# A three-product float32 matmul: both parts of the operand in one product of 512 columns

## The reference

```python
proj = jnp.einsum('bsd,de->bse', h, w_in)                     # 2048 x 15424
q = jnp.einsum('bsr,re->bse', _rmsnorm(q_a, q_a_norm_g), w_q_b)
kv = jnp.einsum('bsr,re->bse', _rmsnorm(c_kv, kv_a_norm_g), w_kv_b)
y_mla = jnp.einsum('bse,ed->bsd', attn * jax.nn.silu(z_mla), w_o_mla)
y_conv = jnp.einsum('bse,ed->bsd', b_gate * conv * jax.nn.silu(z_conv), w_o_conv)
merged = jax.nn.sigmoid(g_mla) * y_mla + jax.nn.sigmoid(g_conv) * y_conv
out = jnp.einsum('bsd,de->bse', merged, w_out)
```

## Time and profile before

| | us |
|---|---|
| median of 3 runs | 2057.07 |
| the profiled execution | 2053.59 |
| its span | 2052.3 |
| TensorE busy in it | 1996.5 |
| TensorE's weight loads busy | 1935.6 |
| VectorE busy | 1167.2 |
| ScalarE busy | 876.5 |
| GpSimd busy | 298.5 |

### The profile page before, as it was taken

One profiled execution on the slowest core, in us unless ns is written; L12 is line 12 of the kernel. 1 busy time (PEld: TensorE's weight loads), 2 busy tenths in 40 slices (PEclk: granted clock), 3 DMA queues, 4 the chain that ended last, 5 costly groups with the idle time before them and its releaser, 6 DMA issues.

```text
span 2052.3 us, 37120 instructions
## 1 busy us (share of the span) xinstructions
PE 1996.5 (97%) x15778; PEld 1935.6 (94%) x15778; DVE 1167.2 (57%) x1727; ACT 876.5 (43%) x1264; POOL 298.5 (15%) x335
## 2 busy tenths in 40 slices
PE   7999999999999999999999699999999999999999
PEld 7999999999999999999999699898999988999987
DVE  5765555555554455644654655476456677564654
ACT  5444454444344334444444433345443333354443
POOL 2110010202010002300211521030011122030200
PEclk9999999999999999999999999999999999999999
DMA  7465454466666566565565364443464443556564
GB/s 238 142 189 174 139 149 144 135 185 184 185 178 185 185 184 180 179 188 184 185 223 183 118 203 134 132 136 113 145 185 134 124 124 115 175 183 190 184 227 159
DMA packets 177695, 343.79 MB, mean 168 GB/s; under 512 B 10478, under 2 KB 19050, under 8 KB 177002
## 3 DMA queue, kind: packets, MB, share of 16 engines
q1 hardware_dynamic: 176154, 337.16, 54.4%
q10 hardware_dynamic: 1376, 4.26, 0.6%
HBM read 335.09 MB, written 6.29 MB: 166 GB/s over the span
## 4 chain that ended last, share of the span: by engine, by line
PE 83%; issue 8%; DVE 2%; POOL 2%; ACT 1%; POOLq 0%; DVEq 0%; ACTq 0%
PE bank L1233 82%; DVE w_lo L1853 1%; POOL arena L2434 1%; ACT w_hi L1556 1%; POOL scratch L2431 1%; DVE arena L2120 0%; POOL arena L2478 0%; POOL stats L2385 0%; DVE head_factor L1890 0%; ACT scratch L1714 0%; DVE ob_lo L2125 0%; DVE arena L2222 0%; ACT ob_hi L1712 0%; POOL acc_a L2365 0%; DVE best L2220 0%
## 5 line engine op out<-in xcount | busy, mean ns | idle before, releaser
L1853 DVE TENSOR_TENSOR w_lo<-w_raw,w_hi 128x1024 fp32r<-128x1024 f32 (+2 forms) x644 | 784.5, 1222 | 800.8 <-ACT w_hi L1556 799.5
L1556 ACT ACTIVATE w_hi<-w_raw 128x1024 fp32r<-128x1024 f32 (+2 forms) x644 | 661.5, 1031 | 935.1 <-PE bank L1233 934.5
L1233 PE MATMUL bank<-hb_hi,w_hi 128*128 128x256 f32 x2448 | 700.1, 286 | 0.0
L1233 PE MATMUL bank<-hb_lo,w_hi 128*128 128x256 f32 x2448 | 694.9, 284 | 0.0
L1233 PE MATMUL bank<-hb_hi,w_lo 128*128 128x256 f32 x2448 | 694.7, 284 | 0.0
L1233 PE MATMUL bank<-ob_hi,w_hi 128*128 128x256 f32 (+1 forms) x2224 | 645.6, 290 | 11.3 <-DVE ob_lo L2125 7.1
L1233 PE MATMUL bank<-ob_hi,w_lo 128*128 128x256 f32 (+1 forms) x2224 | 628.0, 282 | 0.0
L1233 PE MATMUL bank<-ob_lo,w_hi 128*128 128x256 f32 (+1 forms) x2224 | 626.7, 282 | 0.0
L1233 PEld LDWEIGHTS bank<-hb_hi,w_hi 128*128 128x128 f32 x2448 | 471.5, 193 | 6.8 <-DVE w_lo L1853 5.4
L1233 PEld LDWEIGHTS bank<-hb_lo,w_hi 128*128 128x128 f32 x2448 | 471.6, 193 | 0.0
L1233 PEld LDWEIGHTS bank<-hb_hi,w_lo 128*128 128x128 f32 x2448 | 471.3, 193 | 0.0
(11 more groups left out here) (245 smaller groups left out, 1217.0 us busy)
## 6 DMA issues: line engine op xcount, KB each, us to landing
w_raw<-in_w_in SPq DMA_DIRECT2D x436, 512.0 KB, 3.7
w_raw<-in_w_out SPq DMA_DIRECT2D x64, 512.0 KB, 4.1
w_raw<-in_w_o_conv SPq DMA_DIRECT2D x32, 512.0 KB, 3.7
w_raw<-in_w_o_mla SPq DMA_DIRECT2D x32, 512.0 KB, 3.7
w_raw<-in_w_branch SPq DMA_DIRECT2D x32, 512.0 KB, 3.7
w_raw<-in_w_kv_b SPq DMA_DIRECT2D x16, 512.0 KB, 3.9
w_raw<-in_w_q_b SPq DMA_DIRECT2D x16, 384.0 KB, 3.3
arena<-x_kept SPq DMA_DIRECT2D x2, 2048.0 KB, 9.0
```

The lines of the kernel that those rows point to most:

```text
L1233: return nc.tensor.matmul(dst, lhsT, rhs, start=start, stop=stop, skip_group_check=True)
L1556: act(dst, src, ACT.Copy).then_inc(S_("w_hi"), 1)
L1853: tt(low, src, high.bitcast(F32), ALU.subtract).then_inc(S_("w_lo"), 1)
```

## The change

The two operand buffers `hb_hi`, `hb_lo` become halves of one buffer `hb`, likewise `ob`. In the phases marked `wide` (256 tokens and no `hold`) the products hi x hi and hi x lo of an f tile are one product of 512 columns: its moving side is 256 columns of the high part followed by the same 256 of the low part, and it fills a whole bank. The product lo x hi is added to the first half. Token-major tiles, the phases with 272 columns and wout stay. VectorE then adds the two halves of the bank (a TENSOR_REDUCE over pairs, which raises `sum`), waits for it, and multiplies in SBUF as before. `sum` frees the bank, `evac` starts what follows. Where the factor and the result are the same buffer (bgate, oconv, branch_a), the sum goes to a scratch buffer, taken from the ring of five.

```diff
+        self.wide = n == S and not hold
...
-        self.hb_hi, self.hb_lo = sb("hb_hi", [P, KT, S], F32R), sb("hb_lo", [P, KT, S], F32R)
-        self.ob_hi, self.ob_lo = sb("ob_hi", [P, KT, T], F32R), sb("ob_lo", [P, KT, T], F32R)
+        self.hb, self.ob = sb("hb", [P, 2, KT, S], F32R), sb("ob", [P, 2, KT, T], F32R)
+        self.hb_hi, self.hb_lo = self.hb[:, 0, :, :], self.hb[:, 1, :, :]
+        self.ob_hi, self.ob_lo = self.ob[:, 0, :, :], self.ob[:, 1, :, :]
...
+    def both(self, name, k):
+
+        if name in ("h", "mg", "ya", "yb"):
+            return self.hb[:, :, k + 8 * (name == "yb"), :]
+        if name == "h2":
+            return self.ob[:, :, k, NMETA:T]
+        return self.ob[:, :, k + 4 * (name == "lat_kv"), 0:S]
...
-            if kind == "f":
+            if kind == "f" and u.phase.wide:
+                mm(pair(dst), hi_w[:, k, COLS(j)], m.both(u.phase.operand, kt), first, last)
+                inst = mm(dst[:, 0:S], lo_w[:, k, COLS(j)], x_hi, False, last)
+            elif kind == "f":
...
+    def both_by(s, dst, factor, *marks, between=None):
+
+        b, at = m.proj[s.of["pb"]], dst if between is None else between
+        ve.wait_ge(*s.of["got"])
+        for mark in marks:
+            ve.wait_ge(*mark)
+        v.tensor_reduce(at, b.rearrange("p (h x) -> p x h", h=2), AX, ALU.add).then_inc(S_("sum"), 1)
+        ve.wait_ge(*s["sum"])
+        tt(dst, at, factor, ALU.mult).then_inc(S_("evac"), 1)
...
     def gate(s):
         name, k = s.args
         if name in ("gc", "gm"):
-            out_by(s, scratch_of(s), m.R, done["r1"])
+            both_by(s, scratch_of(s), m.R, done["r1"])
...
     def evac_oc(g, m, pb, got):
         k = 4 * g + m
-        done["yc", k] = add("oconv", k, marks="evac", pb=pb, got=got)["evac"]
-        return done["yc", k]
+        sc = scratch.take()
+        s = add("oconv", k, marks="sum evac", pb=pb, got=got, scratch=sc)
+        sc.ends(s["evac"])
+        done["yc", k] = s["evac"]
+        return s["sum"]
```

More of the change, by code:

```diff
@@ L468, in evac @@
             sc = scratch.take() if m else None
-            s = add("latent", which, m, marks="evac sq" + (" sq_acc" if m else ""), pb=pb, got=got, scratch=sc)
+            s = add("latent", which, m, marks="sum evac sq" + (" sq_acc" if m else ""), pb=pb, got=got, scratch=sc)
             if m:
@@ L526, in evac @@
         def evac(g, m, pb, got):
-            s = add("cin", j, m, marks="evac", pb=pb, got=got, free=list(conv_free[m]))
+            s = add("cin", j, m, marks="sum evac", pb=pb, got=got, free=list(conv_free[m]))
             done["cin", m] = s["evac"]
-            return s["evac"]
+            return s["sum"]
         return evac
@@ L534, in evac @@
             sc = scratch.take()
-            s = add("cgate", j, m, marks="evac tap0", pb=pb, got=got, scratch=sc, gate=done["cin", m],
+            s = add("cgate", j, m, marks="sum evac tap0", pb=pb, got=got, scratch=sc, gate=done["cin", m],
                     free=list(conv_free[m]))
@@ L547, in evac @@
         def evac(g, m, pb, got):
-            s = add("bgate", j, m, marks="evac conv_b", pb=pb, got=got, taps=done["taps", m])
+            sc = scratch.take()
+            s = add("bgate", j, m, marks="sum evac conv_b", pb=pb, got=got, taps=done["taps", m], scratch=sc)
+            sc.ends(s["evac"])
             done["conv_b", m] = s["conv_b"]
-            return s["evac"]
+            return s["sum"]
         return evac
@@ L556, in evac @@
             sc, hd = scratch.take(), heads.take()
-            s = add("zconv", j, m, marks="evac sig silu gated", pb=pb, got=got, scratch=sc, head=hd, y=done["conv_b", m])
+            s = add("zconv", j, m, marks="sum evac sig silu gated", pb=pb, got=got, scratch=sc, head=hd, y=done["conv_b", m])
             hd.ends(s["silu"])
@@ L587, in evac @@
             sc = scratch.take()
-            s = add("gate", name, k, marks="evac gate", pb=pb, got=got, scratch=sc, free=list(free))
+            s = add("gate", name, k, marks="sum evac gate", pb=pb, got=got, scratch=sc, free=list(free))
             sc.ends(s["gate"])
             done[name, k] = s["gate"]
-            return s["evac"]
+            return s["sum"]
         return evac
@@ L608, in evac @@
             sc, hd = scratch.take(), ring.take()
-            s = add("z_sig", name, k, marks="evac sig", pb=pb, got=got, scratch=sc, head=hd)
+            s = add("z_sig", name, k, marks="sum evac sig", pb=pb, got=got, scratch=sc, head=hd)
             def gate_y():
@@ L634, in evac @@
             sc = scratch.take()
-            s = add("merge", name, k, marks="evac merged", pb=pb, got=got, scratch=sc, gate=done[gate, k], other=done[other, k])
+            s = add("merge", name, k, marks="sum evac merged", pb=pb, got=got, scratch=sc, gate=done[gate, k], other=done[other, k])
             sc.ends(s["merged"])
@@ L790, in evac_qa2 @@
     def evac_qa2(g, m, pb, got):
-        s = add("qa2", 4 * g + m, marks="evac", pb=pb, got=got)
+        s = add("qa2", 4 * g + m, marks="sum evac", pb=pb, got=got)
         pending.append(qa_job(4 * g + m, s["evac"]))
-        return s["evac"]
+        return s["sum"]
     def token_major(name):
@@ L866, in evac_qb @@
         sc = scratch.take()
[L867 removed]
+        s = add("qb", k, marks="sum evac sig qb", pb=pb, got=got, scratch=sc)
         sc.ends(s["qb"])
         done["qb", k] = s["qb"]
[L870 removed]
+        return s["sum"]
     def recurrence(pr):
@@ L953, in evac_ba @@
         k = 4 * g + m
-        done["pa", k] = add("branch_a", k, marks="evac", pb=pb, got=got)["evac"]
-        return done["pa", k]
+        sc = scratch.take()
+        s = add("branch_a", k, marks="sum evac", pb=pb, got=got, scratch=sc)
+        sc.ends(s["evac"])
+        done["pa", k] = s["evac"]
+        return s["sum"]
     run(ph["ba"], evac_ba)
@@ L2029, in cin @@
         j, t = s.args
-        out_by(s, m.gate_t[:, t, :], m.RR, done["rr"], *[done[key] for key in s.of["free"]])
+        both_by(s, m.gate_t[:, t, :], m.RR, done["rr"], *[done[key] for key in s.of["free"]])
     def cgate(s):
         j, t = s.args
-        out_by(s, scratch_of(s), m.gate_t[:, t, :], s.of["gate"])
+        both_by(s, scratch_of(s), m.gate_t[:, t, :], s.of["gate"])
     def taps(s):
```

62 lines of the change are left out of this document (32 added, 30 removed).

## The result

The changed kernel takes 2164.3 us (median of 4 runs, 2163.5 to 2165.1) against 2056.3 before: 1.052 times, interval 1.051 to 1.054. The forecast was 2096. It has the sign right and the size wrong: 5.2% slower for 1.9%. The profiled span is 2163.6 us.

The account below looks back on a forecast made before the run. TensorE, busy 1996.5 of 2052.3 us, was taken to bound the kernel. Stalls of 74 us minus 33.3 saved gave +41, so 2094 from the profiled 2053.59 and, with the runs' median higher, 2096 us; range 2040 to 2165.

Parts of the forecast that it names:

- the gate group's 0.95 us of stall: At the ends of 12 gconv, gmla and gb groups TensorE stands 0.95 us for a late w_lo: 11.4 us.
- the wait for the third bank: In 24 groups without a sigmoid, the next group's fourth tile waits 0.4 us for the third tile's bank: 9.6 us.
- latents, qb: Four groups with ScalarE behind each evacuation: 4 us of stalls.
- saving of the products: On TensorE two products of 256 columns become one of 512; 4016 change, each saves 0.0083 us, together 33.3 us.
- the sum over the groups: Stalls from VectorE's longer evacuations, mostly at the ends of groups, added over all kinds of group: 74 us.
- z phases: zconv, zmla, zb, 10 groups: 0.95 us of stall plus 0.6 from a later w_lo beside GpSimd: 16 us.
- The recurrence: ga, za, ba, 10 groups mostly beside the recurrence: 1.7 us counted of a burst's 2.8 growth, 17 us.
- The clock: TensorE's granted clock was read as that of 2.4 GHz in all slices (digit 9).
- the third: Rival: VectorE's sum is dearer, 0.93 us, since it steps 256 elements; 66 us more, 2162; chance 0.20.
- The first: Rival: queues absorb the burst, as the sum costs no more than an evacuation now (0.41 us); 2036 us; chance 0.14.
- the second: Rival: gain and loss cancel; wide product at 0.2133 us, 74 us more, half given back; 2059; chance 0.05.
- the fourth: Rival: the wide product on TensorE brings nothing (0.240 us); 33 us more, 2128; chance 0.08.

Follow-up runs that it names:

- e1_products: Changed kernel's products, but the old one-operation evacuation, reading only the first half of the bank; 2034.4 us, 0.990 of the kernel before.
- e3_from_bank: As e4_bank_held, but the multiplication reads the bank's first half, so the sum is made but left out of the result; 2139.8 us, 1.041.
- e4_bank_held: As the changed kernel, but the bank is freed by the multiplication and not by the sum; 2171.0 us, 1.056 of the kernel before.
- e5_narrow_rec: As the changed kernel, but with the change taken back in ga, za and ba, the phases beside the recurrences; 2139.7 us, 1.041.

## Why the prediction was wrong

Right were: the pitch of the wide product in layer 1, the sum (0.68 us for 0.67), the evacuation's 1.06 us, the gate group's 0.95 us of stall, the wait for the third bank (0.57 for 0.4, oconv), VectorE's busy time, TensorE's waits for `w_lo` (53.8 us for some 50), and that a gain on TensorE is lost on VectorE at the ends of groups. Lateness against e1_products, by the kinds of the sum:

| kind | forecast | measured |
|---|---|---|
| gconv, gmla, gb | 11.4 | 17.0 |
| zconv, zmla, zb | 16 | 29.7 |
| cgate | 8 | 5.5 |
| latents, qb | 4 | 12.2 |
| cin, bgate, oconv, omla, bb, qi, qa2 | 9.6 | 20.0 |
| q | 8 | 12.4 |
| ga, za, ba | 17 | 29.8 |
| saving of the products | -33.3 | -21.6 |

The kinds of the table add up to 127 us; the other phases and the start bring it to 130.

The step that failed is the sum over the groups: 74 us of stalls, measured 130 in spans. The mechanism, a longer burst ahead of `w_lo` in strict queues, was right; four of its terms were too small, and the clock was put at nothing.

- **z phases, and what they hand on.** "Shifted, and with about 0.4 us because the multiplication now reads SBUF twice beside GpSimd": the mechanism was seen and counted once a group. It is paid at every meeting, three times 0.5 us in a zmla group. The second zmla group stood 4.3 us longer than with the products alone, for 1.6. The runs split this: 1.1 us are there without the slow multiplications (24.05 us in e3_from_bank against 22.98), 1.7 come with them (25.75 in e4_bank_held), and 1.6 with the lower clock, which e4_bank_held does not have there. The first gconv, gmla and gb groups carry some of the lateness: 23.72 us against 21.56 in gconv, while the inner groups stand 0.9 to 1.5 us for the forecast 0.95.
- **The recurrence.** "Of the 2.8 us that a burst grows I count 1.7: 17. Ends of this choice: 0 and 28." It was 29.8, just above my upper end; ga's groups stood 2.6 to 6.1 us each. I had bounded the term by the burst's growth. A step of the recurrence that starts late also leaves TensorE idle, and behind the idle the clock is lower. Here is the end of ga's last group, VectorE and then TensorE:

```profile
1735.65 0.42 DVE L1997 TENSOR_TENSOR scratch<-scratch,factor 128x256 f32<-128x256 f32 x1
1737.50 1.23 DVE L1877 TENSOR_TENSOR w_lo<-w_raw,w_hi 128x1024 fp32r<-128x1024 f32 x1 [1.43 <-ACT w_hi L1580]
1738.64 0.72 DVE L2339 COPY_PREDICATED arena<-small,bank 128x256 f32<-128x256 uint8 x1
```
```profile
1739.71 1.94 PE L1254 MATMUL bank<-arena 128*128 128x64 f32 x8 [4.12 <-issue]
1741.41 0.77 PE L1254 MATMUL bank<-ob,w_hi 128*128 128x512 f32 x1
1741.98 0.41 PE L1254 MATMUL bank<-ob,w_lo 128*128 128x256 f32 x1
1742.19 0.63 PE L1254 MATMUL bank<-ob,w_hi 128*128 128x512 f32 x1
1742.62 0.41 PE L1254 MATMUL bank<-ob,w_lo 128*128 128x256 f32 x1
```

  The burst, the sigmoids, `w_hi`, `w_lo` and only then the recurrence's own COPY_PREDICATED: TensorE's next product starts only behind that one and has stood 4.12 us.
- **Latents, qb, and the phases that wait for a bank.** 19 us more than forecast in the two kinds. The multiplications of the latents and of qb too meet GpSimd (6.5 us of e4_bank_held against e3_from_bank), and that was not costed. In oconv the wait for a bank came out near the forecast (0.57 us for 0.4); why cin, bgate and qa2 stand longer stays open, as do the 4 us by which q is over.
- **The products.** The saving was 0.0083 us each from one phase's pace, and 0.0054 in the mean: 12 us. Of the Trainium skill ("TensorE: Matmul & The Clock Gate", Back-to-back issue gap) the prediction gave the formula alone: the page calls it the gap of a product by itself and says that in a stream, where each product has its weight load, it is off in both directions. So it did not decide the matter; the measured mean lies between its 0.0025 us and my 0.0083.
- **The clock.** It was read as full from the digit 9 and put at nothing. The granted clock of the profiled execution is 0.979, and 0.991 in e1_products. I estimate what that costs from the products that start in the stretches at 1.2 GHz, at 0.417 us more for 1000 columns (the difference between the two levels): 31 us in the changed kernel, 13 in e1_products and 7 in the kernel before. So some 18 of the 130 us are the clock's; they lie inside the terms above and are not to be added to them.

56 us of stalls and 12 of saving make the 68 between 2096 and 2164. Of the rivals, the third gave 2162, near the measured time, for a reason that did not happen: its sum of 0.93 us was 0.68. It was luck, not a right rival. That the range reached just far enough (2165) is owed to that rival and supports no step. The first, queues that absorb the burst, was ruled out by the gate groups; the second (74 us saved) and the fourth (nothing saved) by the 21.6 us of e1_products.

## What to carry to other kernels

An operation added at an evacuation is paid where the queues are strict: ask what stands behind it on its engine, and if it is the feed of TensorE, issue only what frees the bank there and the rest behind the feed; the order alone gave back 87 of 108 us here. A cost met at every tile beside another engine is counted per meeting, not per group, and a pace taken from one phase is checked in each phase it is used for. Where a chain runs through several engines, a wait can cost more than its length: behind TensorE's longer idles its clock was at the lower level, so look at the granted clock by short windows and not by the digits of the page.

## What the runs showed of the hardware

- VectorE's multiplication of two SBUF operands (256 columns) takes 0.42 us alone and 0.91 to 0.95 us while GpSimd multiplies in SBUF; with one operand in PSUM it takes 0.424 us in the mean beside the same GpSimd work. That is worth 31 us of this kernel (e4_bank_held against e3_from_bank).
- A TENSOR_REDUCE that adds the elements of a bank 256 apart takes 0.681 us for 512. The contiguous reductions of the earlier trace rows give 0.652 by their 0.95 ns an element, so the stride cost at most 0.03 us. Four of them back to back take 2.48 us.
- After the 4.12 us idle above, TensorE's products ran at half pace: pairs 0.64 us apart (1741.98 to 1742.62 and on to 1744.54) instead of 0.35, the clock's lower level of 1.2 GHz, until 1744.75. Five pairs so cost 1.5 us on top of the idle. In zmla a wait of 1.99 us, with one of 0.58 us 5.7 us earlier, was followed by the same half pace; in e4_bank_held waits of 0.57, 0.59 and 1.02 us were not. The granted clock of 1600 to 1800 us was 0.92; it was 0.98 in e5_narrow_rec:

```profile
1600.00:1800.00 200.00, 175.64 (x1031) 154.04 (x1030) 138.46 (x239) 59.57 (x83) 30.53 (x39) 0.92 0.38 114
```

(columns: window, us, busy us and count of PE, PEld, DVE, ACT and POOL, granted clock, DMA share, GB/s; the changed kernel). In the changed kernel six such stretches lie between 1600 and 1830 us.
